# Permuting a turned block on the way into DRAM instead of on the way back

## The reference, cut to what matters

```python
# first block
proj = einsum('bsd,de->bse', rms_norm(x), w_in)       # q, k, v, z of three branches, gates
qa = rope(qa); ka = rope(ka); ya = moba_attention(qa, ka, va) * silu(za)
qb = rope(qb); kb = rope(kb); yb = dilated_mixture(qb, kb, vb) * silu(zb)
ym = memory_attention(qm, mk, mv) * silu(zm)          # mk, mv = rms_norm(mem) @ w_mem_kv
merged = g_a * (ya @ w_proj_a) + g_b * (yb @ w_proj_b) + g_m * (ym @ w_proj_m)
x = rms_norm(x + merged @ w_out)
# second block
lru_x, lru_g, q, k, v, ret_g = split(rmsnorm(x) @ w_in2)
h = x + concat([rg_lru(conv(lru_x)) * gelu(lru_g), retention(q, k, v, ret_g)]) @ w_out2
h = h + (silu(u @ w_gate) * (u @ w_up)) @ w_down      # u = rmsnorm(h)
out = rmsnorm(h)
```

## Time and profile before

| | us |
|---|---|
| median of 3 runs | 2201.22 (2200.91 to 2202.69) |
| the profiled execution | 2200.99 |
| its span, first to last instruction | 2199.2 |
| PE busy | 2183.5 |
| DVE busy | 1303.1 |
| ACT busy | 1027.7 |
| POOL busy | 144.6 |

### The profile page before, as it was taken

How to read it: one execution, slowest core, us unless ns; L and a number is a source line. 1 busy time by engine, 2 the same in 40 slices (tenths; PEclk the granted TensorE clock), 3 DMA queues, 4 the chain that set the end, 5 groups by cost and what they waited for, 6 DMA issues and landing times.

```text
span 2199.2 us, 26113 instructions
## 1 busy us (share of the span) xinstructions
PE 2183.5 (99%) x9906; PEld 1810.7 (82%) x9906; DVE 1303.1 (59%) x1559; ACT 1027.7 (47%) x1235; POOL 144.6 (7%) x242
## 2 busy tenths in 40 slices
PE   8999999999999999999999999999999999999998
PEld 7888888888888888888888888888888888888886
DVE  5755656676455645546676888665555555554544
ACT  5544444444444444444555666454444444444443
POOL 0010101011000000000111100110001000100000
PEclk9999999999999999999999999999999999999999
DMA  8775656577754657667778756676777777776664
GB/s 290 220 231 174 204 170 211 183 227 233 211 160 151 213 179 227 202 207 280 231 255 253 227 185 192 199 246 207 216 213 224 216 211 215 229 227 199 194 195 145
DMA packets 228674, 464.65 MB, mean 211 GB/s; under 512 B 16345, under 2 KB 16609, under 8 KB 227681
## 3 DMA queue, kind: packets, MB, share of 16 engines
q1 hardware_dynamic: 212128, 408.73, 59.4%
q0 software_dynamic: 15712, 53.49, 8.0%
q10 hardware_dynamic: 736, 1.12, 0.1%
HBM read 437.59 MB, written 25.69 MB: 211 GB/s over the span
## 4 chain that ended last, share of the span: by engine, by line
PE 95%; DMA 2%; DVE 2%; issue 1%; ACT 1%; POOL 0%; SPq 0%; POOLq 0%; ACTq 0%; DVEq 0%
PE ps L1483 30%; PE ps L1485 30%; PE ps L1484 30%; DMA stage<-bounce 1%; PE ps L1374 1%; PE ps L1396 1%; PE ps L1343 1%; DVE w_lo L864 1%; DMA bounce<-tmp 0%; DMA raw<-in_w_mem_kv 0%; PE ps L1385 0%; ACT w_hi L578 0%; DVE tmp L1025 0%; POOL stage L521 0%; DVE stage L1020 0%
## 5 line engine op out<-in xcount | busy, mean ns | idle before, releaser
L864 DVE TENSOR_TENSOR w_lo<-raw,w_hi 128x1024 fp32r<-128x1024 f32 (+1 forms) x776 | 931.6, 1211 | 765.3 <-ACT w_hi L578 764.2
L578 ACT ACTIVATE w_hi<-raw 128x1024 fp32r<-128x1024 f32 (+1 forms) x776 | 811.6, 1052 | 912.3 <-PE ps L1485 826.0
L1483 PE MATMUL ps<-w_hi,xT_hi 128*128 128x512 f32 x1088 | 430.1, 395 | 0.4 <-DVE w_lo L864 0.4
L1485 PE MATMUL ps<-w_hi,xT_lo 128*128 128x512 f32 x1088 | 424.2, 390 | 0.0
L1484 PE MATMUL ps<-w_lo,xT_hi 128*128 128x512 f32 x1088 | 423.6, 389 | 0.0
L1483 PE MATMUL ps<-w_hi,u2T_hi 128*128 128x512 f32 x704 | 274.0, 389 | 0.0
L1485 PE MATMUL ps<-w_hi,u2T_lo 128*128 128x512 f32 x704 | 273.9, 389 | 0.0
L1484 PE MATMUL ps<-w_lo,u2T_hi 128*128 128x512 f32 x704 | 273.9, 389 | 0.0
L1485 PEld LDWEIGHTS ps<-w_hi,xT_lo 128*128 128x128 f32 x1088 | 204.2, 188 | 43.2
L1483 PEld LDWEIGHTS ps<-w_hi,xT_hi 128*128 128x128 f32 x1088 | 204.4, 188 | 42.5 <-DVE w_lo L864 1.9
L1484 PEld LDWEIGHTS ps<-w_lo,xT_hi 128*128 128x128 f32 x1088 | 204.5, 188 | 41.0
(11 more groups left out here) (262 smaller groups left out, 2250.0 us busy)
## 6 DMA issues: line engine op xcount, KB each, us to landing
raw<-in_w_in SPq DMA_DIRECT2D x368, 512.0 KB, 4.4
raw<-in_w_ffn_gate SPq DMA_DIRECT2D x88, 512.0 KB, 4.3
raw<-in_w_ffn_up SPq DMA_DIRECT2D x88, 512.0 KB, 4.5
raw<-in_w_ffn_down SPq DMA_DIRECT2D x88, 512.0 KB, 4.6
raw<-in_w_out SPq DMA_DIRECT2D x64, 512.0 KB, 5.1
bounce<-tmp POOLq DMA_DIRECT2D x41, 512.0 KB, 3.3
stage<-bounce POOLq DMA_DIRECT2D x164, 128.0 KB, 5.3
raw<-in_w_mem_kv SPq DMA_DIRECT2D x32, 512.0 KB, 5.9
```

What stands on the lines that cost most here:

```text
L578: nc.scalar.activation(w_hi[:, s, 0:per], raw[:, s, 0:per], ACT.Copy).then_inc(hi_ready, 1)
L864: nc.vector.tensor_tensor(w_lo[:, s, 0:per], raw[:, s, 0:per], w_hi[:, s, 0:per].bitcast(F32), ALU.subtract)\
L1483: nc.tensor.matmul(bank(2 * par + t), x_hi, w_hi[:, s, k], start=first, stop=False)
L1485: ins = nc.tensor.matmul(bank(2 * par + t), x_lo, w_hi[:, s, k], start=False, stop=last)
```

## The change

The permutation moves from the reads to the write. `tmp` is written in four DMAs, one for each quarter q of its partitions, and each puts its eight pieces of 512 B per partition where the reader will want them: row `32 m + a`, column `(t, q)`. Then one DMA reads `bounce` to `stage`, 4 KB to a partition. `b_out` now counts 64 for each trip and `b_in` 16, and the waits for them (POOL, ACT's `use_late`, ACT's squares of x) are changed to match.

```diff
@@ -512,14 +512,14 @@
                 for b in range(first - 1, last):
                     pool.wait_ge(z_made, b + 1)
                     if b:
-                        pool.wait_ge(b_in, 64 * b)
-                    pool.dma_start(bounce, tmp[:, :, :].rearrange("p t n -> p (t n)")).then_inc(b_out, 16)
-                    pool.wait_ge(b_out, 16 * (b + 1))
+                        pool.wait_ge(b_in, 16 * b)
+                    for q in range(4):
+                        pool.dma_start(bounce.rearrange("(m a) (t q x) -> q a t m x", a=32, t=NT, q=4)[q],
+                                       tmp[32 * q:32 * (q + 1), :, :].rearrange("p t (m x) -> p t m x", m=4)).then_inc(b_out, 16)
+                    pool.wait_ge(b_out, 64 * (b + 1))
                     if squares:
                         pool.wait_ge(sq_done, squares + b + 1 - first)
-                    for m in range(4):
-                        pool.dma_start(stage[32 * m:32 * (m + 1), :, :].rearrange("p t (q x) -> p t q x", q=4),
-                                       bounce.rearrange("(q a) (t m x) -> m a t q x", a=32, t=NT, m=4)[m]).then_inc(b_in, 16)
+                    pool.dma_start(stage[:, :, :].rearrange("p t n -> p (t n)"), bounce).then_inc(b_in, 16)
@@ -716,7 +716,7 @@
-                    act.wait_ge(b_in, w.times("b", 64, 1))
+                    act.wait_ge(b_in, w.times("b", 16, 1))
@@ -783,7 +783,7 @@
-            four[1]["act_hooks"] = {7: [lambda: act.wait_ge(b_out, 16),
+            four[1]["act_hooks"] = {7: [lambda: act.wait_ge(b_out, 64),
                                         lambda: squares(x_tok, sumsq_x, lambda t: act.wait_ge(in_x[t], 16 * QUAD))]}
```

## The result

The changed kernel takes 2224.1 us (median of 4 runs, 2221.07 to 2224.86). The kernel before, run beside it, takes 2201.26 us (4 runs, 2200.91 to 2202.69). The ratio is 1.0098, with a 95% interval of 1.0084 to 1.0111. The forecast was 2201.0 with a range of 2200.0 to 2204.0, so it was wrong by 23 us and in its sign. The profiled execution took 2224.86 us with a span of 2223.1, against 2200.99 and 2199.2 before, so 23.9 us are to be found.

The account below looks back on a forecast made before the run. The prediction took PE's matmuls to bound the kernel, busy 2183.5 of 2199.2 us. From 2200.99 it took 0.2 for a shorter trip, giving 2200.8, then added 0.23 for the runs' median: 2201.0, range 2200.0 to 2204.0.

Parts of the forecast that it names:

- The write leg: In each trip, from first write issued to the read's issue: issues 1.8, landing 5.3, step 0.3 us.
- The read: In each trip, the single 512 KB read from DRAM to stage was to land in 5.0 us.
- the sum of 12.4: Whole new round trip through DRAM, writes plus read: 12.4 us, against 13.3 and 12.6 before.
- d: Change in the length of one round trip through DRAM, forecast at -0.5 us, ends about -4.5 and +7.
- The three `kbT` waits: ACT's waits for turned k blocks were to total within 14.3 +- 3 us after the change.
- The feed-forward stage, the residual tiles and `mrgT_hi`: Trips with cover: feed-forward free until d is near 3, `mrgT_hi` alike, residual tiles adding d - 1 above 1 us.
- The fourth trip of the k tiles: Trip behind the q/k stretch, with some 0.8 us of cover; adds d - 0.8 above 0.8 us.
- 3d: Cost in the turned q/k stretch if d is positive: three trips on the chain, no slack at its end.
- signs of being wrong: Last q/k write over 7 us, PE idle microseconds at 520, 543 or 559, or time moving with middle windows full.
- PE never waits for that trip directly: Whole kernel: only ACT waits for the trip; its delay reaches PE through splits, `w_lo` and the four weight slots.
- the 5.9 us of the prediction: Feed-forward weight slots: about 5.9 us to spare after split and subtraction, before PE needs the refilled slot.
- The slower rival: Scattered writes land late in the q/k stretch, d = +2, costing 8.2 us, so 2209; much later had chance 0.11.

Follow-up runs that it names:

- e7: Changed kernel with four plain writes (4 KB pieces) instead of the scattering ones, permutation left out so it computes something else; 2210.62 us, ratio 1.0040.
- e10b: Kernel before, with one POOL fill of tmp between the write's landing and the reads in trips 7 to 11; 2208.19 us, ratio 1.0032.
- e4: Changed kernel, but in tiles with a softmax unit ACT takes the trip's result behind the exponentials, not three splits ahead; 2208.67 us, ratio 1.0031.
- e6: Kernel before with its one plain write cut into four plain writes of 32 partitions, reads unchanged; 2233.30 us, ratio 1.0138.
- e9: Kernel before, with four POOL fills of tmp between the write's landing and the reads in trips 7 to 11; 2234.36 us, ratio 1.0146.
- e5: Changed kernel, but for trips 5 to 12 SP holds back weight loads until the trip's writes have landed; 2209.50 us, ratio 1.0029.
- e11: Changed kernel with both edits: ACT takes the trip's result behind the exponentials, and SP holds weight loads until the writes land; 2211.47 us, ratio 1.0045.
- e3: Kernel before with the new form (four writes, one read) in trips 5 to 11 only; 2220.42 us, ratio 1.0087.

## Why the prediction was wrong

*Right.* The write leg was forecast at 1.8 + 5.3 + 0.3 = 7.4 us and took 7.3 to 8.1 in trips 5 to 13 and 6.8 in the median from trip 15 on. The read was forecast at 5.0 and took 5.3 and 5.6 in trips 12 and 13 and 5.1 in the stages behind them. For the trips of the earlier trace rows the sum of 12.4 stands against 13.1 and 13.0 measured, so d was -0.2 and +0.4 there. The three `kbT` waits fell in the band named. The feed-forward stage, the residual tiles and `mrgT_hi` cost nothing. The fourth trip of the k tiles was to add d - 0.8: it took 15.1 us instead of 13.4, so 0.9, and PE stands 1.13.

*First failed step: d was taken from the wrong trips.* "the trip changes by d = -0.9 and -0.2 us; say d = -0.5" came from two trips in the chain, of 13.3 and 12.6 us. A chain shows the occurrences that somebody waited for; they are no sample of the 41. In trips 7 to 11 the old trip took 10.1 us in the median, and its reads are issued in a pause of the loads: in trip 7 they go out from 339.36, and SP issues no load between 337.80 and 341.83. Landings of the four reads between 300 and 500 us in the kernel before:

```profile
DMA to landing us min/median/max: 3.1/3.7/5.3
```

Landings of the one read there in the kernel after:

```profile
DMA to landing us min/median/max: 6.7/6.9/8.1
```

The new write leg ends 4.3 us later, and the read goes out among the next loads: in trip 7 at 342.56, between loads issued at 341.93 and 343.34. The busy share of the DMA engines does not tell the two apart, it is 1.00 in the reads' window before (339.3 to 346.4) and 0.90 in the read's after (342.5 to 350.7). So d is +4.7 there, and +3.8 in trip 11, the first of the three that the prediction would have paid 3d for; PE stands 2.66 us behind it at 520 us, which was one of its signs of being wrong. Even the 12.4 that was forecast would have been +2.3, and by e7 and e10b, which have such a length, some 7 us slower.

*Second failed step: "PE never waits for that trip directly".* Literally true, but the prediction concluded that only weights and their four slots stand between the trip and PE. ACT works in order: behind the late copy stand the splits and the softmax exponentials. This second path has a cover of 1.0 us (0.7 at 377), and a third one behind it, from the exponentials over DVE to `y_tok`, has none. The slots had the 5.9 us of the prediction, which ACT's wait of 5.95 in trip 7 used up. e4 shows that the order on ACT matters, since it changes nothing else and takes 16 us of the loss away; trip 7 and e10b show which waits end last.

*Third, not foreseen at all: the clock.* At the stands of 4.23, 3.68, 3.14 and 2.66 us, within 1.2 us of their end, the granted clock fell to half. A window of the second such stretch:

```profile
385.60:389.00 3.40, 3.30 (x10) 2.72 (x11) 2.06 (x2) 2.49 (x5) 0.00 (x0) 0.50 0.14 46
```

That turned 18.4 us of stands into some 24.

*The rivals.* The slower rival had the mechanism (the scattered writes land late, beside the loads) and a chance of 0.11. It placed it in the k tiles and priced it at 8.2 us. In the k tiles it came to 2.66 us at trip 11 and 1.13 at trip 14.

*Left open.* Why the reads of e6 need 9.0 us is not settled; that they start later is what e9 shares with it. How much of the loss each of the three paths takes was read from single trips and not separated by an experiment. The own cost of held loads in e5 and e11 was followed only as far as ACT's waits. The 2.9 and 1.4 us for splitting and for 512-byte pieces beside the burst are differences of medians of two kernels, not a measurement of either by itself.

## What to carry to other kernels

When a step recurs, take its old duration from every class of its occurrences, not from the ones that the chain shows: here it was 13 us in the chain and 10 in the class that decided. For an in-order engine, count the cover of everything queued behind its wait, not of the one product that you follow: here that was 5.9 us for the weights, 1.0 for the exponentials and nothing for what DVE makes from them. And a transfer's landing belongs to the moment of its issue: one that starts 4 us later can meet a burst of loads that the old one missed.

## What the hardware showed that was not expected

The granted clock fell from 1.00 to 0.50 at single stands of 2.66 to 4.23 us in a PE otherwise full, four times in the kernel after, and matmuls of the same shape then started 0.43 us apart instead of 0.227. In e4, whose stands are at most 1.34 us, it stayed up. Between these the length of the stand does not decide alone: in e3 the clock fell at a stand of 2.06 us (488) and not at one of 2.82 (356), after stayed up at 2.24 (490), and e6 at 3.35 (464). By the granted clock these are the two levels of 1.2 and 2.4 GHz. The Trainium skill ("TensorE: Matmul & The Clock Gate", Part 1) names these two levels and ties them to how busy the engine has been; the trace agrees with the factor, 0.43 / 0.227 = 1.9.

Four requests of 128 KB beside the weight loads took a write leg of 7.85 us, against 4.86 with the loads held. The one request of 512 KB, issued 0.8 us ahead of the first load of the burst (335.82 against 336.66 in trip 7 before), landed in 3.3, against 2.9 alone. Splitting a short transfer into four moved its last parts behind the first loads (335.62 in trip 7 after).
